# Score copies on ScalarE, and gate vectors spread inside the first chunk's merge

## Time and profile before

| | us |
|---|---|
| median of 3 runs (5702.1 to 5712.31) | 5704.44 |
| the profiled execution's own time | 5690.06 |
| its span, first to last instruction | 5688.3 |
| TensorE matmul busy | 4484.2 (79%) |
| VectorE busy | 3691.5 (65%) |
| GpSimd busy | 1597.8 (28%) |
| ScalarE busy | 890.1 (16%) |

### The profile page before, as it was taken

One profiled execution on the slowest core, in us unless ns is written; L12 is line 12 of the kernel. 1 busy time (PEld: TensorE's weight loads), 2 busy tenths in 40 slices (PEclk: granted clock), 3 DMA queues, 4 the chain that ended last, 5 costly groups with the idle time before them and its releaser, 6 DMA issues.

```text
span 5688.3 us, 47082 instructions
## 1 busy us (share of the span) xinstructions
PE 4484.2 (79%) x14736; PEld 2602.6 (46%) x14736; DVE 3691.5 (65%) x8127; ACT 890.1 (16%) x2536; POOL 1597.8 (28%) x1310
## 2 busy tenths in 40 slices
PE   4999997799788666666669999967897976766675
PEld 3766686344443222222248666854444432222222
DVE  0565415788677888876517554166886878888765
ACT  1023301111111111111110232011111111111111
POOL 0000000343334454445300000003442334444552
PEclk8999998899899888888879999989997998888887
DMA  6100042799988999999851001428998899999996
GB/s 248 60 30 1 18 156 100 304 379 371 372 349 348 422 421 421 421 420 421 332 212 52 30 1 45 144 110 330 384 372 348 353 363 421 421 421 421 420 421 283
DMA packets 226377, 1585.28 MB, mean 279 GB/s; under 512 B 26064, under 2 KB 28368, under 8 KB 46672
## 3 DMA queue, kind: packets, MB, share of 16 engines
q0 software_dynamic: 184320, 1342.26, 58.2%
q1 hardware_dynamic: 41808, 240.02, 11.2%
HBM read 1579.03 MB, written 3.15 MB: 278 GB/s over the span
## 4 chain that ended last, share of the span: by engine, by line
PE 39%; DMA 34%; DVE 17%; issue 3%; ACT 3%; DVEq 2%; POOL 1%; SPq 0%; POOLq 0%; ACTq 0%
DMA B<-tables,R 17%; PE ps L476 8%; DMA A<-tables,R 7%; PE ps L486 5%; PE ps L596 5%; DMA H<-tables,R 4%; DVE A L1426 4%; DVE B L1394 3%; DMA B<-ws 3%; PE ps L581 2%; PE ps L493 2%; PE ps L506 2%; PE ps L701 2%; DVE A L1394 2%; PE ps L688 2%
## 5 line engine op out<-in xcount | busy, mean ns | idle before, releaser
L476 PE MATMUL ps<-B,A 128*128 128x512 f32 x2048 | 1166.8, 716 | 544.8 <-ACT A L868 544.3
L444 POOL DMA_INDIRECT B<-tables,R x716 | 875.8, 1223 | 1837.0 <-PE ps L476 787.3
L1394 DVE SCALAR_TENSOR_TENSOR B<-B,M 128x1024 f32<-128x1024 f32 x716 | 867.5, 1225 | 295.8 <-DMA B<-tables,R 268.0
L476 PEld LDWEIGHTS ps<-B,A 128*128 128x128 f32 x2048 | 441.2, 225 | 1191.5 <-ACT A L868 672.2
L476 PE MATMUL ps<-A 128*128 128x512 f32 x992 | 536.5, 676 | 159.7 <-ACT A L868 159.6
L486 PE MATMUL ps<-H,B 128*128 128x384 f32 (+1 forms) x2048 | 593.1, 444 | 66.4 <-DMA B<-ws 44.9
L444 POOL DMA_INDIRECT A<-tables,R x356 | 441.9, 1241 | 583.7 <-PE ps L476 367.7
L486 PEld LDWEIGHTS ps<-H,B 128*128 128x128 f32 x2048 | 398.9, 195 | 258.2 <-DMA B<-ws 49.9
L1394 DVE SCALAR_TENSOR_TENSOR A<-A,M 128x1024 f32<-128x1024 f32 x356 | 433.6, 1224 | 123.7 <-DMA A<-tables,R 111.6
L862 ACT ACTIVATE T<-T 128x2 f32<-128x2 f32 (+1 forms) x448 | 92.5, 206 | 2357.9 <-DVEq L1396 2346.4
L476 PEld LDWEIGHTS ps<-A 128*128 128x128 f32 x992 | 211.4, 221 | 455.6 <-issue 237.1
(11 more groups left out here) (206 smaller groups left out, 5067.5 us busy)
## 6 DMA issues: line engine op xcount, KB each, us to landing
B<-ws SPq DMA_DIRECT2D x120, 1024.0 KB, 5.1
B<-ws SPq DMA_DIRECT2D x128, 768.0 KB, 4.7
B<-tables,R POOLq DMA_INDIRECT x716, 22.2
A<-tables,R POOLq DMA_INDIRECT x356
R<-tabs SPq DMA_DIRECT2D x2, 2176.0 KB, 8.7
H<-tables,R POOLq DMA_INDIRECT x192, 20.2
x<-xin SPq DMA_DIRECT2D x1, 2560.0 KB, 9.0
y<-M SPq DMA_DIRECT2D x1, 2560.0 KB, 7.9
```

Source lines behind the costliest of these rows:

```text
L444: pool.indirect_dma_start(out=ring[s], out_offset=None, in_=tables[:, :], in_offset=bass.IndirectOffsetOnAxis(ap=EI[:, n:n + 1], axis=0),) ...
L476: mm = pe.matmul(ps[:, bk + c, :], diag[PE_AT[n] % DIAGS], v_row[:, c * 512:(c + 1) * 512], start=(n % SLOTS == 0), stop=(PE_AT[n] + 1 == ...
L1394: v.scalar_tensor_tensor(out=u_row, in0=u_row, scalar=1.0, in1=h2[:, g.tile, :], op0=ALU.mult, op1=ALU.mult, accum_out=dots[:, o:o + 1])
```

## The change

Two things are moved. The score copies go from VectorE to ScalarE in both chunks: in chunk 0 ScalarE copies a unit's products after the next unit's query copy; in chunk 1 it does so between two expert groups, after the next unit's query copy. VectorE keeps a wait at the place where it copied. And the 8 gate pieces go inside chunk 0's merge: VectorE makes the first diagonal ahead of the merge and the others after steps 2, 6, ... 26, TensorE multiplies and ScalarE copies after steps 1, 5, ... 29, through banks 4 and 5 in place of 0 and 1. VectorE waits for all 8 before the residual that uses them.

```diff
 TensorE
-                for i in range(8):
+                def gate_rows(i):
                     pe.wait_ge(rw_dg.sem, rw_dg.at(l, i + 1))
                     pe.wait_ge(rw_ev.sem, rw_ev.at(l, i - 1))
-                    pe.matmul(ps[:, i % 2, :], onesD, T[:, 0:512], start=True, stop=True).then_inc(rw_ps.sem, 1)
-                pe.wait_ge(rw_ev.sem, rw_ev.at(l, 8))
+                    pe.matmul(ps[:, 4 + i % 2, :], onesD, T[:, 0:512], start=True, stop=True).then_inc(rw_ps.sem, 1)
...
                     mix_gates(l, 0, s)
                     mix_branch(l, 0, s)
+                    if s % 4 == 1:
+                        gate_rows(s // 4)
 ScalarE
+            def score_copy(l, c, hp):
+                o = hp * P
+                act.wait_ge(pq_sp.sem, pq_sp.at(l, c * UNITS + hp + 1))
+                both = (A[:, 0:4096], B2[:, 2048:6144])[c].rearrange("p (t n) -> p t n", t=2)
+                last = act.copy(both[:, :, o:o + P], ps[:, 2 + hp % 2, 0:2 * P].rearrange("p (t n) -> p t n", n=P))
+                if c:
+                    last = act.copy(KS[4][:, o:o + P], ps[:, 2 + hp % 2, 2 * P:3 * P])
+                last.then_inc(pq_s.sem, 1)
...
                 for s in range(N_MG):
                     sigmoid(l, 0, s)
+                    if s % 4 == 1:
+                        gate_rows(s // 4)
...
                 for hp in range(UNITS):
                     query_copy(l, 0, hp)
+                    if hp:
+                        score_copy(l, 0, hp - 1)
+                score_copy(l, 0, UNITS - 1)
...
                     experts(l, AT_KEYS + hp * KEY_STEP)
                     query_copy(l, 1, hp)
+                    if hp:
+                        score_copy(l, 1, hp - 1)
                     experts(l, AT_KEYS + hp * KEY_STEP + 1)
+                score_copy(l, 1, UNITS - 1)
 VectorE
                 def score_copy(c, hp):
-                    o = hp * P
-                    v.wait_ge(pq_sp.sem, pq_sp.at(l, c * UNITS + hp + 1))
-                    both = (A[:, 0:4096], B2[:, 2048:6144])[c].rearrange("p (t n) -> p t n", t=2)
-                    last = v.tensor_copy(both[:, :, o:o + P], ps[:, 2 + hp % 2, 0:2 * P].rearrange("p (t n) -> p t n", n=P))
-                    if c:
-                        last = v.tensor_copy(KS[4][:, o:o + P], ps[:, 2 + hp % 2, 2 * P:3 * P])
-                    last.then_inc(pq_s.sem, 1)
+                    v.wait_ge(pq_s.sem, pq_s.at(l, c * UNITS + hp + 1))
...
+                gate_diagonals(0)
                 for s in range(N_MG):
                     mix(0, s)
+                    if s % 4 == 2 and s < N_MG - 4:
+                        gate_diagonals(s // 4 + 1)
+                v.wait_ge(rw_ev.sem, rw_ev.at(l, 8))
```

More of the change, by code:

```diff
@@ L876, in _ @@
             act.sem_inc(rw_ev.sem, 2)
+            act.sem_inc(pq_s.sem, 2)
             act.wait_ge(cst_in.sem, 7 * 16)
@@ L1004, in _, with gate_rows @@
                     attention(t + 1, t)
-                for i in range(8):
+                def gate_rows(i):
                     act.wait_ge(rw_ps.sem, rw_ps.at(l, i + 1))
-                    act.activation(grow[:, i // 4, (i // 2) % 2, (i % 2) * 512:(i % 2 + 1) * 512], ps[:, i % 2, :],
+                    act.activation(grow[:, i // 4, (i // 2) % 2, (i % 2) * 512:(i % 2 + 1) * 512], ps[:, 4 + i % 2, :],
                                    ACT.Copy, scale=float(CONV) * (0.5 if i < 4 else 1.0)).then_inc(rw_ev.sem, 1)
@@ L1078, in _ @@
             v.sem_inc(mg_ev.sem, 2)
-            v.sem_inc(pq_s.sem, 2)
+            pass
             v.sem_inc(pe_used.sem, DIAGS)
@@ L1263, in _, with gate_diagonals @@
                     attention(t + 1, t)
-                for i in range(8):
+                def gate_diagonals(i):
                     if i:
```

## The result

The changed kernel takes 5664.41 us (median of 4 runs, 5662.25 to 5666.71) against 5708.38 (4 runs, 5702.10 to 5716.31) for the kernel before, a ratio of 0.9922 with a 95% interval of 0.9905 to 0.9940. A second set gave 5664.41 (5 runs) against 5693.37 (11 runs), 0.9943 [0.9927, 0.9959]. The forecast was 5673 us, range 5655 to 5692. So the gain is 29 to 44 us for 31 forecast.

A forecast was written before the change was run, and what follows sets the result against it. Bounds by stage: TensorE the merge, VectorE chunk 0's selection, a loop through several engines chunk 1's units, DMA the last stage. 2 x (6.9 + 5.6 + 3) = 31 us off the 5704.44 median gave 5673 us, range 5655 to 5692.

The forecast's parts named there:

- Part 1: Chunk 0's merge: starts 13.76 us earlier, takes in 6.88 us of gate matmuls; net 6.9 us a layer (6.2 to 6.9).
- Part 2: Chunk 0's selection: VectorE loses the score copies, 0.80 us for each of 7 heads; 5.6 us a layer (5.3 to 6.0).
- ScalarE kept up: Chunk 0: ScalarE's units take 7.8 us a head, below VectorE's 10.5, so VectorE's new wait is met before it is reached.
- the early finish: TensorE ends chunk 0's units near 967, chunk 1's first merge matmuls start over 20 us early, and this buys nothing.
- Part 3: Chunk 1's units: VectorE loses 0.72 us of copies a unit, ScalarE's gelu comes later; 3 us a layer gained.
- The queue delay: Chunk 1's even units: two score copies ahead of the gelu in ScalarE's in-order queue start it 0.8 us later.
- The count that the forecast starts from: Chunk 1's units in the kernel before: 2 of 7 pairs in each layer are of the fast kind.
- the share of fast pairs: Chunk 1 after the change: 3 of 7 pairs taken as fast, 24.8 us against 26.6 slow; which kind wins was left open.
- A: Chunk 1's loop gives the whole 0.72 us a unit or settles fast: 10 to 11.5 us a layer, 5658 us; chance 0.20.
- B: Chunk 1: all pairs slow, ScalarE's queue eating all that VectorE gains, 2 us a layer lost; 5683 us; chance 0.18.
- C: Merge or selection edit fails: gate matmuls cost as much as before, or ScalarE's hand-over paces selection; about 12 us, 5692; chance 0.09.
- D: Chunk 1's merge: TensorE stays at half clock after 30 us without work; slower, 5761 us; chance 0.05.

The follow-up runs named there:

- gelu first: The changed kernel, but in chunk 1's even steps ScalarE makes the second group's gelu ahead of the score copies: 5653.79 us, 0.9923 against the kernel before.
- the four with filling: Unused extra matmuls at the end of the last attention: kernel before 1.0042, changed 0.9953; half as many: before 0.9975, changed with gelu first and chunk 1 matmuls 0.9937.
- the second profile: The kernel before, unchanged, run and profiled again: 5702.88 us, 1.0001 against 30 runs of the kernel before.
- with the idle filled: The changed kernel with six unused extra matmuls in the odd steps of chunk 1's units: 5667.89 us, 0.9942 against the kernel before.

## Why the prediction was right

**Time and sign.** 5664.41 for 5673, by the mechanisms forecast. That 31 us lies next to the measured 29 to 44 is in part luck: in the two profiles the three terms come to 25, 6 short, and a cause that the forecast doesn't have, the clock of the chain, adds up to 20. The steps:

**Part 1, the merge.** The start (0.06 us behind the copy) and the eight matmuls (0.86 each) came as worked out, and at full clock the term is exact (174.03 = 167.15 + 6.88; the forecast's 173 took the window of 166 us for the merge). What failed is taking both ends from one execution. The 13.76 us that go are 21.25 in executions whose chain runs at half clock; and without the chain the merge's first 16 passes may be those that run at half clock, up to 2.5 us back. So the stretch saves 4.6 to 6.9 us a layer against an execution like the first profile, and 190.7 - 176.1 = 14.6 against one like the second. With chunk 0's 5 and chunk 1's 2.7, two layers give 2 x 12.5 = 25 in the one case and 2 x 22.3 = 45 in the other, which spans the measured 29 to 44. So the clock of the chain can account for the 19 us that the two profiles don't show. How many of the timed executions had it at half clock isn't known, so that it does account for all of them is not shown. The sentence "nothing in the terms depends on that difference", on the 14 us between the profiled execution and the median, was wrong: this chain alone differs by 15 us between the two profiled executions of the kernel before.

**Part 2.** 4.6 to 5.1 us a layer for 5.6: 0.72 a head (11.33 before, 10.61 now) rather than 0.80, since 0.25 us of idle stay where the copies and a gap of 0.09 us were; a few heads take 0.3 us more in either kernel, hence 4.6 in one layer and 5.1 in the other. ScalarE kept up, TensorE's units came 3.90 apart, chunk 1's merge began at 968.18 (967 forecast), and the early finish bought nothing, all as said.

**Part 3.** -2.5 and -2.9 for -3, with pairs of 26.50 and 24.82 (26.6 and 24.8 forecast), 5 of 12 of them fast (3 of 7 taken). The queue delay is 0.73 for 0.8. The count that the forecast starts from is too high: of the six pairs from odd multiply to odd multiply in each layer of the kernel before, one is fast (25.84 and 26.03 us), and the others take 26.3 to 26.8, not two of seven. So the pairs gain more than said, 4.5 and 3.7 us a layer, and the end of the stretch gives some back; that the term is met within 0.5 us is partly chance, as is the share of fast pairs, which the forecast called open. The two experiments on it (VectorE copying in even steps, and gelu first) show the balance of the forecast, gain on VectorE against delay on ScalarE, from both sides. The Trainium skill, "PSUM — Partial Sum Buffer", section "Engine vs sequencer instructions", has ScalarE's queue strictly in order; the trace agrees, the gelu at 1656.12 behind the copies and at 1716.88 once they are put after it.

**Rivals.** A (all pairs fast) and B (all slow) are out by the pairs. C is out by the 0.86 us matmul and the 10.61 us head. D is out: full clock was back 7.2 us after the idle of 29.21, and 6.8 us after the one of 6.39. The Trainium skill's page "TensorE: Matmul & The Clock Gate", section "What's actually happening", by which activity releases the half clock, agrees there.

**Open.** What makes the clock fall at the end of attention in one execution and not in the next is not shown. The ten profiles without filling pass there 20 times, 10 of them at half clock; the four with filling pass 8 times, none at half clock. The rest of the spread was not traced to a place. It goes with the clock: over the 30 runs of the kernel before, the mean granted clock falls from 0.903 in the shortest (5680.74 us) to 0.893 in the longest (5722.33), which is more than the chain can make: by an estimate from the second profile, two stretches of 190.7 us at a mean of 0.93 in place of 1.00 take 0.005 off the mean of 5700 us. And the gelu-first kernel, which has no chain, spreads 29 us in 6 runs, so the small spread of the changed kernel does not show that the chain was its cause.

## What to carry to other kernels

Before taking a duration from one profile into a sum, look whether the stretch runs at a clock that another execution may not grant: the head of the merge, a chain of short matmuls with waits between them, cost 13.8 or 21.3 us here. Moving work from a busy engine to an idle one pays only in the stretches that the busy engine sets; split a loop at the hand-overs, and put the moved work in the idle engine's queue behind what others wait for, not ahead of it.

## What was not expected of the hardware

- After the same 2.58 us of idle, TensorE's next eight passes took 5.40 us at one place of the changed kernel (1670.93 above) and 3.70 at another (below); with the idle filled, the whole stage ran at a granted clock of 1.00 instead of 0.96.

```profile
4480.03 3.70 PE L476 MATMUL ps<-A 128*128 128x512 f32 x8 [2.58 <-ACT A L880]
```

- A matmul of 384 f32 columns against a 128x128 f32 identity takes two passes of 0.32 us at full clock: fillers cost twice what one pass would suggest.
- ScalarE copies 128 columns out of the banks in 0.27 us and 256 in 0.37, so most of a small copy is its fixed part.
- Two waits that are met before they are reached, between two drains, left 0.25 us of idle on VectorE, where 0.09 had stood behind a copy.
